# Second attention of a two-block transformer: scores two pairs ahead in the second accumulator, probabilities normalized before their transposes, whole filler units

## The reference

```python
def _sink_softmax(scores, sink):
    m = jnp.maximum(jnp.max(scores, axis=-1, keepdims=True), sink)
    e = jnp.exp(scores - m)
    return e / (jnp.sum(e, axis=-1, keepdims=True) + jnp.exp(sink - m))
...
    o_a = _windowed_attention(q_a, k_a, v_a, k_a_c, v_a_c, sink.reshape(A_KV_HEADS, A_GROUPS))
    o_b = _global_attention(q_b, jnp.concatenate([k_b, k_b_c], axis=1), jnp.concatenate([v_b, v_b_c], axis=1))
    return _merge_branches(o_a, o_b, proj[..., OFF_GA:], w_branch_a, w_branch_b, w_out)
...
def _merge_branches(o_a, o_b, gate_logits, w_branch_a, w_branch_b, w_out):
    g_a, g_b = jnp.split(jax.nn.sigmoid(gate_logits), 2, axis=-1)
    return (g_a * (o_a @ w_branch_a) + g_b * (o_b @ w_branch_b)) @ w_out
```

## Time and profile before

| | |
|---|---|
| time before, median of 3 runs | 920.03 us (919.59 to 920.88) |
| profiled execution | 920.46 us |
| its span on the core | 918.8 us |
| mean granted TensorE clock | 0.999 |
| TensorE busy | 898.8 us, 98% of the span, 4732 matmuls |
| VectorE busy | 721.5 us, 79% |
| ScalarE busy | 550.9 us, 60% |
| GpSimd busy | 161.8 us, 18% |
| DMA | 176.20 MB at a mean of 192 GB/s |

### The profile page before, as it was taken

How to read it: one execution, slowest core, us unless ns; L and a number is a source line. 1 busy time by engine, 2 the same in 40 slices (tenths; PEclk the granted TensorE clock), 3 DMA queues, 4 the chain that set the end, 5 groups by cost and what they waited for, 6 DMA issues and landing times.

```text
span 918.8 us, 13753 instructions
## 1 busy us (share of the span) xinstructions
PE 898.8 (98%) x4732; PEld 729.9 (79%) x4732; DVE 721.5 (79%) x1046; ACT 550.9 (60%) x863; POOL 161.8 (18%) x247
## 2 busy tenths in 40 slices
PE   8999999999999999999999999999999999999996
PEld 6888888777878788888888887666688688888885
DVE  4779466878878788888778798865578889999976
ACT  6775755476775576777333345755664766666633
POOL 8000100215600000110112001740000033344400
PEclk9999999999999999999999999999999999999999
DMA  9746843876653457887699665322245455555572
GB/s 322 205 146 198 288 136 119 280 267 209 182 165 116 133 170 256 276 281 252 215 326 344 195 193 191 88 81 92 71 157 190 142 174 183 181 174 174 176 248 77
DMA packets 100537, 176.20 MB, mean 192 GB/s; under 512 B 8560, under 2 KB 36592, under 8 KB 100352
## 3 DMA queue, kind: packets, MB, share of 16 engines
q1 hardware_dynamic: 93120, 149.87, 51.0%
q0 software_dynamic: 7184, 25.50, 8.4%
q10 hardware_dynamic: 176, 0.08, 0.0%
HBM read 174.38 MB, written 1.05 MB: 191 GB/s over the span
## 4 chain that ended last, share of the span: by engine, by line
PE 59%; DVE 4%; ACT 2%; issue 1%; DMA 1%; DVEq 0%
PE acc L783 41%; PE acc L1160 3%; PE acc L1165 2%; PE scores L1160 2%; PE turned L1160 2%; PE turned L1269 2%; PE scores L1258 1%; PE turned L875 1%; PE turned L1371 1%; DVE wlo L1951 1%; PE turned L1165 1%; PE scores L1165 1%; PE turned L1185 1%; PE turned L819 1%; DMA raw<-in_w_out 1%
## 5 line engine op out<-in xcount | busy, mean ns | idle before, releaser
L1951 DVE TENSOR_TENSOR wlo<-raw,whi 128x1024 fp32r<-128x1024 f32 (+3 forms) x269 | 346.7, 1308 | 89.1 <-ACT whi L1411 78.7
L1411 ACT CAST whi<-raw 128x1024 fp32r<-128x1024 f32 (+3 forms) x269 | 273.2, 1032 | 151.4 <-PE acc L783 97.3
L783 PE MATMUL acc<-whi,lta 128*128 128x512 f32 (+2 forms) x896 | 228.0, 392 | 0.2 <-DVEq L2528 0.2
L783 PEld LDWEIGHTS acc<-whi,lta 128*128 128x128 f32 x896 | 160.2, 188 | 43.4 <-issue 11.2
L783 PE MATMUL acc<-wlo,lta 128*128 128x512 f32 (+2 forms) x448 | 121.2, 383 | 0.0
L665 POOL DMA_DIRECT2D wm<-in_w_mod x48 | 34.4, 719 | 420.8 <-DVEq L2082 237.4
L783 PEld LDWEIGHTS acc<-wlo,lta 128*128 128x128 f32 x448 | 82.9, 188 | 16.9
L783 PE MATMUL acc<-whi,ltb_hi 128*128 128x512 f32 (+1 forms) x268 | 73.2, 391 | 1.4 <-ACT ltb_hi L1864 0.8
L783 PE MATMUL acc<-whi,ltb_lo 128*128 128x512 f32 (+1 forms) x268 | 71.5, 385 | 0.2 <-DVE ltb_lo L2784 0.2
L783 PE MATMUL acc<-wlo,ltb_hi 128*128 128x512 f32 (+1 forms) x268 | 71.0, 383 | 0.0
L783 PEld LDWEIGHTS acc<-whi,ltb_lo 128*128 128x128 f32 x268 | 49.3, 188 | 11.4 <-DVE ltb_lo L2784 1.5
(11 more groups left out here) (387 smaller groups left out, 1440.6 us busy)
## 6 DMA issues: line engine op xcount, KB each, us to landing
raw<-in_w_in SPq DMA_DIRECT2D x88, 512.0 KB, 4.1
wm<-in_w_mod POOLq DMA_DIRECT2D x48, 512.0 KB, 6.4
raw<-in_w_up SPq DMA_DIRECT2D x88, 256.0 KB, 3.0
raw<-in_w_up SPq DMA_DIRECT2D x32, 512.0 KB, 4.7
raw<-in_w_down SPq DMA_DIRECT2D x32, 512.0 KB, 5.0
raw<-in_w_down SPq DMA_DIRECT2D x44, 256.0 KB, 3.3
raw<-in_w_o SPq DMA_DIRECT2D x8, 512.0 KB, 4.7
raw<-in_w_out SPq DMA_DIRECT2D x8, 512.0 KB, 3.9
```

Of the source, the lines that this page charges most:

```text
L783: ins = pe.matmul(acc[s][:, t, 0:n], lhs[part][:, kt0 + kk, tok], w[:, u % RING, kk, 0:n], start=(opens and k == 0 and kk == 0 and j == 0) ...
L1411: act.copy(whi[:, s, :, 0:n], raw[:, s, :, 0:n]).then_inc(hi_ready, 1)
L1951: dve.tensor_tensor(wlo[:, s, :, 0:n], raw[:, s, :, 0:n], whi[:, s, :, 0:n].bitcast(F32), ALU.subtract)\
```

## The change

In the attention the panels IN3 to IN6 and BA0 all go to `acc[0]`, and `acc[1]` serves as two more banks for scores. So four score tiles can stand, and TensorE issues S(p+2) in pair p. VectorE divides the probabilities by their sums in SBUF (`ab_norm`: for each pair two small instructions and two of 128x512) before TensorE transposes them; the two inverse products and VectorE's two instructions on V(p) go. V(p−1) follows S(p+2), and ScalarE and VectorE split it right out of PSUM into `ltb` (`ab_hi`, `ab_low`) pair by pair. The filler comes as one whole unit per pair, three units ahead instead of two. ScalarE casts ahead of its exps, and VectorE's splits lag one unit behind ScalarE's casts. Probabilities and their transposes get a second buffer, and GpSimd's squares for B get their own (`ab_squares`). SP's and GpSimd's instructions keep their order.

```diff
+BESIDE_SCORES = ("IN3", "IN4", "IN5", "IN6", "BA0")
...
+            s = 0 if name in BESIDE_SCORES else i % 2
+            self.banks[name] = s, filled[s]
+            filled[s] += 1
...
+AB_LATE = 6
...
-AB_LAST = 2
+AB_LAST = 1
...
-    return min((4 * KT + 2 * KT // 2) // UNIT - AB_LAST, j + 2)
+    return min((4 * KT + 2 * KT // 2) // UNIT - AB_LAST, j + 3)
...
+    b = i % 4
+    S_USE[f"AB.{i}"] = b, i // 4 + MLA_SCORES.get(b, 0)
...
+        sc += [acc[1][:, t] for t in range(T)]
...
+            def ab_turned(p):
+                for e in range(2):
+                    pe.wait_ge(ev("ab_normed"), 2 * p + e + 1)
+                    bank, full = t_begin(f"AB.PT{2 * p + e}")
+                    for j in range(4):
+                        ins = pe.transpose(bank[:, P * j:P * j + P], ab_prob[p % 2][:, e, P * j:P * j + P], ident[:])
+                    ins.then_inc(full, 1)
...
-                pe.wait_ge(ev("ab_sums"), p + 1)
-                for e in range(2):
-                    ins = pe.matmul(bank[HD * e:HD * e + HD, P:2 * P],
-                                       soft[:, (2 * p + e) % 4, 8:9].broadcast_to([P, HD]), ident[:],
-                                    start=True, stop=True)
...
+            ab_scores(0)
+            s, k = PLAN.bank("IN2")
+            pe.wait_ge(panel_out[s], k + 2)
+            ab_scores(1)
+            ab_fill(0)
+            for p in range(AB_PAIRS):
+                ab_turned(p)
+                if p + 2 < AB_PAIRS and p != AB_LATE:
+                    ab_scores(p + 2)
                 if p > 0:
-                    ab_turn(p - 1, 0)
-                ab_fill(p, (1,))
-            attend_pairs("AB", AB_PAIRS, ab_scores, 4, ab_values, lambda p: ab_fill(p, (0,)), after=lambda p: ab_turn(p, 1),
-                         fill_rest=ab_rest)
-            ab_unit(18)
+                    ab_values(p - 1)
+                ab_turn(p)
+                ab_fill(p + 1)
+                if p == AB_LATE:
+                    ab_scores(p + 2)
+            ab_values(AB_PAIRS - 1)
...
+                act.wait_ge(t_full[b], k + 1)
+                act.copy(ltb[0][:, 4 * br + hp, P * t:P * t + P], tb[b][:, 0:P])\
+                   .then_inc(lt_hi if p % AB_SPAN == AB_SPAN - 1 else ev("oab_hi"), 1)
...
+            ahead(PLAN.unit["IN3"])
+            ab_exp(0)
+            ahead(PLAN.unit["IN3"] + 1)
+            ab_exp(1)
+            ahead(PLAN.unit["IN3"] + 2)
+            sqrt("ab", stat[:, 2:4, :])
+            for p in range(AB_PAIRS):
+                for e in range(2):
+                    t_out(f"AB.PT{2 * p + e}", ab_probT[p % 2][:, e, :])
+                ahead(PLAN.unit["IN3"] + ab_units(p))
+                if p > 0:
+                    ab_hi(p - 1)
+                ab_out(p)
+                if p + 2 < AB_PAIRS:
+                    ab_exp(p + 2)
+            ahead(PLAN.unit["IN3"] + ab_units(AB_PAIRS))
+            ab_hi(AB_PAIRS - 1)
...
-                done(dve.tensor_copy(inverse_row[:], bank[:, P:2 * P]))
-                return dve.tensor_tensor(oabT[:, 4 * br + h // 2, P * t:P * t + P], bank[:, 0:P], inverse_row[:], ALU.mult)
...
+            def ab_norm(p):
+                for e in range(2):
+                    b, k = S_USE[f"AB.{2 * p + e}"]
+                    dve.wait_ge(s_free[b], k + 2)
+                s = ab_rows(p)
+                if p < AB_PAIRS // 2:
                     done(dve.tensor_tensor(s[:, :, 4:5], s[:, :, 4:5], s[:, :, 6:7], ALU.add))
                 done(dve.reciprocal(s[:, :, 8:9], s[:, :, 4:5]))
-                dve.sem_inc(ev("ab_sums"), 1)
-            def ab_weigh(p, rows, bank):
-                br, h, t = ab_step(2 * p)
-                done(dve.tensor_copy(inverse_row[:], bank[:, P:2 * P]))
-                return dve.tensor_tensor(oabT[:, 4 * br + h // 2, P * t:P * t + P], bank[:, 0:P], inverse_row[:], ALU.mult)
-            def oab_lo(g):
-                dve.wait_ge(lt_hi, lt_done("oab", g))
-                dve.tensor_tensor(ltb[1][:, 2 * g:2 * g + 2, :], oabT[:, 2 * g:2 * g + 2, :],
-                                  ltb[0][:, 2 * g:2 * g + 2, :].bitcast(F32), ALU.subtract).then_inc(lt_ready, 1)
-            def ab_inverse(i):
-                if i == 1:
-                    inverse("ab", stat[:, 2:4, :])
-                    dve.sem_inc(ev("ab_inverse"), 1)
-            def ab_after(i):
-                if i == 0:
-                    for t in range(T):
-                        dve.wait_ge(ev("ab_sq"), t + 1)
-                        norm_sums(t)
-                    var(stat[:, 2:4, :], HD).then_inc(ev("ab_var"), 1)
-                elif i == 2:
-                    done(dve.scalar_tensor_tensor(x3c[:, 0:8], modc[:, 32:40], 1.0, ln1c[:, 0:8], ALU.add, ALU.mult))
-                    done(dve.scalar_tensor_tensor(x3c[:, 8:16], modc[:, 32:40], 1.0, ln1c[:, 8:16], ALU.add, ALU.mult))
-                    done(dve.tensor_tensor(x3c[:, 8:16], x3c[:, 8:16], modc[:, 24:32], ALU.add))
-                elif i == AB_PAIRS // 2 - 1:
-                    dve.wait_ge(ev("qB_normed"), 1)
-                if i % AB_SPAN == 0 and i > 0:
-                    oab_lo(i // AB_SPAN - 1)
-                if i in IN_DONE:
-                    c = IN_DONE.index(i)
-                    biased(f"IN{3 + c}", gate2[:, :, COLS * c:COLS * c + COLS])
+                for e in range(2):
+                    row = ab_prob[p % 2][:, e, :]
+                    dve.tensor_scalar(row, row, s[:, e, 8:9], None, ALU.mult).then_inc(ev("ab_normed"), 1)
...
+            def ab_low(p):
+                br, hp, t = p // (HEADS // 2 * T), p % (HEADS // 2 * T) // T, p % T
+                if p % AB_SPAN == AB_SPAN - 1:
+                    dve.wait_ge(lt_hi, lt_done("oab", p // AB_SPAN))
+                else:
+                    dve.wait_ge(ev("oab_hi"), p + 1 - p // AB_SPAN)
+                b, k = T_USE[f"AB.O{p}"]
+                hi, lo = (v[:, 4 * br + hp, P * t:P * t + P] for v in ltb)
+                dve.tensor_tensor(lo, tb[b][:, 0:P], hi.bitcast(F32), ALU.subtract).then_inc(t_free[b], 1)
+                if p % AB_SPAN == AB_SPAN - 1:
+                    dve.wait_ge(t_free[b], k + 2)
+                    dve.sem_inc(lt_ready, 1)
...
+            ahead(PLAN.unit["IN3"])
+            ab_maxima(0)
+            norm_sums(0)
+            ab_norm(0)
+            ahead(PLAN.unit["IN3"] + 1)
+            norm_sums(1)
+            var(stat[:, 2:4, :], HD).then_inc(ev("ab_var"), 1)
+            ab_maxima(1)
+            for p in range(AB_PAIRS):
+                if p in IN_DONE:
+                    c = IN_DONE.index(p)
+                    biased(f"IN{3 + c}", gate2[:, :, COLS * c:COLS * c + COLS])
+                if p + 1 < AB_PAIRS:
+                    ab_norm(p + 1)
+                if p == 0:
+                    inverse("ab", stat[:, 2:4, :])
+                    dve.sem_inc(ev("ab_inverse"), 1)
+                ahead(PLAN.unit["IN3"] + ab_units(p) - 1)
+                if p == AB_LATE:
+                    ab_low(p - 1)
...
+                if p > 0 and p != AB_LATE:
+                    ab_low(p - 1)
```

203 lines of the change are left out of this document (98 added, 105 removed).

## The result

| | before | after |
|---|---|---|
| median | 920.14 us (919.59 to 920.88, 4 runs) | 933.87 us (932.65 to 936.94, 4 runs) |
| ratio | | 1.0156 [1.0144, 1.0168] |
| profiled execution, span | 920.46, 918.8 us | 936.94, 935.3 us |
| S(0) to the merged branches' first transposes | 127.30 us | 140.22 us |

What follows compares the result with a forecast made beforehand. The prediction took TensorE's issue and waits as the bound. Its terms, −12.4 + 8.4 + 6.4 + 6.1 + 1.2 = +9.7 us on the profiled 920.46, gave 930.2, as a median 929.8 us, range 925.5 to 934.5.

Steps and rivals of the forecast that it cites:

- What goes: TensorE's attention pairs: shorter pairs save 8.2 us over 16 pairs and 4.2 of existing waits vanish, −12.4 us in all.
- The pair becomes 5.84: A plain pair on TensorE falls to 5.84 us, .51 less, with the whole unit taken as 2.84 and V .93.
- Today's waits: TensorE's short waits in pairs 2 and 5 to 11, for exps of the same round: 4.2 us, all to go.
- The start, 8.4 us: First pairs: TensorE waits .4 at S(1), 1.1 at PT(1), 3.1 each at V(0) and unit 4, .7 at PT(2).
- VectorE beside GpSimd, 1.2: Pairs 2 to 5: new normalizing instructions lose time to GpSimd's work on B; 1.2 us taken, bounds 0 and 5.
- rival A: Pairs 2 to 5: VectorE loses to GpSimd at every encounter and sets the pace; 933.6 us, chance .12.
- Rival D: Start: the clock halves behind the new 3 us waits, so some 3 us of matmuls take twice as long; 932.8, chance .04.
- Panel changes, 6.4 us: Pairs 5, 9, 13: TensorE waits 2.0, 2.0 and 2.4 us for PT's evictions, cast, split and emptying, a 5.4 us chain.
- Rival B: Panel changes: no wait if ScalarE's cast of unit p+5 starts 2.0 us sooner; 914.9 us, faster, chance .09.
- Rival C: Full pair gain, start costs 4, panels 6.4, no follow-ons: 919.4 us, no change, chance .05.
- Follow-ons, 6.1 us: Later waits: 3.7 around pairs 6 and 7, .2 after pair 9, .8 after pair 13, 1.4 at the first BB0 unit.
- Sum: Whole kernel: −12.4 + 8.4 + 6.4 + 6.1 + 1.2 = +9.7 us, giving a median of 929.8.

Runs made afterwards that it cites:

- x3: The changed kernel, but GpSimd starts its work on B's norm about 11 us later; 933.02 us, ratio to before 1.0150.
- x1_no_lead: The changed kernel, but VectorE empties IN3 to IN6 without first making the splits of three more units; 925.9 us, ratio to before 1.0069.
- y2: x1_no_lead without GpSimd's work on branch B's norm and rotation, a probe only; 921.11 us, ratio to before 1.0004.
- x2: The changed kernel, but TensorE writes pair 3's scores and pair 0's values four times; 934.0 us, ratio to before 1.0142.
- w1: x1_no_lead, but TensorE writes the scores of pair 3 three times; 925.88 us, ratio to before 1.0056.
- y4_cast_first: The changed kernel, but in pairs 1, 5, 9 and 13 ScalarE casts the next unit ahead of PT's evictions; 927.43 us, ratio to before 1.0074.
- y1: x1_no_lead with ScalarE's and VectorE's order at the start rearranged and the first sigmoid ahead of the last output's cast; 923.26 us, ratio to before 1.0034.
- z1: y1, but VectorE takes ab_low(0) right behind norm(2), ahead of a split and maxima(3); 922.95 us, ratio to before 1.0030.

## Why the prediction was right, and where its sizes were off

- **What goes.** One size was off: "The pair becomes 5.84". It is 5.93, so 6.7 go instead of 8.2; the unit takes 2.88 for my 2.84, between my two rows, and V 1.03 for .93. Today's waits are gone but for .4 in pair 4.
- **The start, 8.4 us.** The waits came where they were put, at S(1), PT(1), V(0) and unit 4; only PT(2)'s .7 did not. Their sizes did not hold: by the sum PT(3) starts 35.6 us behind S(0) (PT(0) at 11.0, three pairs of 5.84 of which one has no V, and 8.0 of waits), measured are 39.0. Of these 3.5 us V(0)'s wait has .8 (3.9 from start to start, for 3.1) and unit 4's .7 (3.8 for 3.1, with V(0) at its usual .93); unit 4 and PT(2) at half the clock have 2.4 and .4; PT(1) and PT(2) give .9 back. The stretched splits account for the two longer waits: in x3, without them, V(0) starts 1.0 and unit 4 2.0 us sooner.
- **VectorE beside GpSimd, 1.2.** Too low, and not in the place foreseen. The new instructions were to pay, and some did (1.71 for two at 604.87, .88 alone), but the splits on the chain paid first, 2.0 us by unit 4 (x3). The whole cost in the changed kernel was not measured; in x1_no_lead it is 3.4 (y2). My row against rival A was no evidence: when the split at 611.03 took 1.22, GpSimd's last instruction, at 607.74, had ended at 608.5. Rows with both at work go either way: a split took 1.53 at 604.73, and one took 1.23 at 590.37, where a product of GpSimd took 1.30 instead of .32.
- **Rival D** came true beside the forecast, where I had held them apart and given it .04. Against it I had set the clock of 1.00 through today's waits, but the longest of these is .7, which says nothing of 3.8. Its price of 3 us was its matmuls' time, and 2.9 came; x2 and w1 show that VectorE's chain covers part of it or all.
- **Panel changes, 6.4 us.** 1.6, 1.6 and 2.1 measured, 5.4; x1_no_lead and y4_cast_first show the mechanism. Rival B's condition, a cast 2.0 us sooner, did not hold in the changed kernel. y4 makes it true in pairs 9 and 13 (2.3 and 2.9 sooner from PT's start), and the waits go as it said; in pair 5, where the cast is 1.1 sooner, .4 is left. Rival C, half of it, did not come.
- **Follow-ons, 6.1 us.** 1.3 at PT(6) (1.2 forecast), .4 and .2 at V(5) and the tile (1.3), 1.1 at V(6) (1.2), .3 after pair 9 (.2), .8 after pair 13 (.8), 1.3 at BB0 (1.4): 5.4.
- **Sum.** 9.7 forecast, 12.9 in the region. The longer pair and the wait in pair 4 add 1.9, the start 2.2 more than its 8.4 and GpSimd's 1.2 together; the panels give 1.0 back and the follow-ons .7. That leaves .8 which I can't place. The direction, the mechanism of the waits and the range held; the size is 4.1 us short between the medians. That 933.87 still lies in the range, .6 below its end, is in part luck: a price that was held to be a rival's came on top, and terms that were too large took some of it off.
- **Rival A** had the engine right, VectorE as the bound of the first pairs, and its cause only in part: x1, w1, y1 and z1 show VectorE's own order and load, GpSimd is 3.4 us on top of it (y2).

Why the change did not win, as far as rows tell: of a pair's 5.93 us in branch A, VectorE is busy with norm 1.3, split 1.2, maxima 2.4 and low part .3, 5.2 before any encounter with GpSimd; before it was 4.6 of 6.35. This is worked out from rows, and z1's give-back fits it; a kernel with less on VectorE in these pairs was not tried. What the last 2.4 us between z1 and before are made of, beside the start, stays open.
